# Two edits to a five-layer transformer stack on one core: other byte addresses for rows and weights, and one weight split moved ahead of each norm

## The reference

```
def rmsnorm(x, g):
    y = x * rsqrt(mean(x * x, -1) + 1e-6)
    return y * g
for i in range(4):
    h = rmsnorm(x, norm_mix_g[i])
    x = x + mixer_i(h)                       # h @ w_in ... @ w_out
    x = x + swiglu(rmsnorm(x, norm_ffn_g[i]), f_w13[i], f_w2[i])
# second block, on concat([meta, x])
h = h + mixer2(rmsnorm(h, norm_mix_w_2))     # h @ w_in (5792 columns)
h = h + swiglu(rmsnorm(h, norm_ffn_w_2), w_gate, w_up, w_down)
out = rmsnorm(h, norm_final_w)[:, 16:]
```

## Time and profile before

| | us |
|---|---|
| three runs | 1760.92, 1771.78, 1774.52 (median 1771.78) |
| the profiled execution, its own time | 1752.1 |
| its span, first to last instruction | 1750.3 |
| TensorE busy | 1691.5 (97%), mean granted clock 0.991 |
| VectorE busy | 1227.7 (70%) |
| ScalarE busy | 971.9 (56%) |
| HBM read | 288 MB, 165 GB/s over the span |

### The profile page before, as it was taken

How to read it: one execution, slowest core, us unless ns; L and a number is a source line. 1 busy time by engine, 2 the same in 40 slices (tenths; PEclk the granted TensorE clock), 3 DMA queues, 4 the chain that set the end, 5 groups by cost and what they waited for, 6 DMA issues and landing times.

```text
span 1750.3 us, 37337 instructions
## 1 busy us (share of the span) xinstructions
PE 1691.5 (97%) x13776; PEld 1599.1 (91%) x13776; DVE 1227.7 (70%) x2013; ACT 971.9 (56%) x1352; POOL 12.9 (1%) x20
## 2 busy tenths in 40 slices
PE   7999999999999999999999999999999999999997
PEld 7999999888999987569999999999999876799997
DVE  6887766586777587888776678776566665577764
ACT  4467745365775454206774446775454645468742
POOL 0000200000000000000000000000000000000000
PEclk9999999999999999999999999999999999999999
DMA  6567674433766554105666456667454432256662
GB/s 206 167 206 240 192 230 139 160 109 97 252 198 223 164 166 141 64 1 158 204 199 213 158 170 183 205 193 250 154 180 145 137 140 61 73 165 198 194 225 70
DMA packets 79545, 290.15 MB, mean 166 GB/s; under 512 B 9739, under 2 KB 12140, under 8 KB 79340
## 3 DMA queue, kind: packets, MB, share of 16 engines
q1 hardware_dynamic: 79468, 289.11, 52.2%
HBM read 288.03 MB, written 1.05 MB: 165 GB/s over the span
## 4 chain that ended last, share of the span: by engine, by line
PE 84%; DVE 11%; ACT 2%; issue 2%; DVEq 0%; DMA 0%; SPq 0%; ACTq 0%
PE bank L570 24%; PE bank L572 23%; PE bank L571 23%; DVE wlo L1516 3%; PE bank L858 2%; PE bank L845 1%; PE bank L799 1%; DVE conv_cv L1625 1%; DVE rinv L1522 1%; PE bank L954 1%; DVE hy_z L1765 1%; PE bank L1050 1%; ACT whi L1148 1%; PE bank L1060 1%; PE bank L1023 1%
## 5 line engine op out<-in xcount | busy, mean ns | idle before, releaser
L1148 ACT CAST whi<-raw 128x1024 fp32r<-128x1024 f32 (+1 forms) x490 | 539.3, 1102 | 328.4 <-PE bank L572 293.0
L570 PE MATMUL bank<-xq_h,whi 128*128 128x256 f32 x2384 | 666.9, 280 | 8.2 <-DVE wlo L1516 8.1
L571 PE MATMUL bank<-xq_h,wlo 128*128 128x256 f32 x2384 | 660.4, 277 | 0.0
L572 PE MATMUL bank<-xq_l,whi 128*128 128x256 f32 x2384 | 660.4, 277 | 0.0
L1516 DVE TENSOR_TENSOR wlo<-raw,whi 128x1024 fp32r<-128x1024 f32 (+1 forms) x491 | 629.9, 1283 | 5.4 <-ACT whi L1148 2.7
L570 PEld LDWEIGHTS bank<-xq_h,whi 128*128 128x128 f32 x2384 | 448.2, 188 | 19.3 <-DVE wlo L1516 12.7
L571 PEld LDWEIGHTS bank<-xq_h,wlo 128*128 128x128 f32 x2384 | 447.8, 188 | 1.5 <-issue 1.5
L572 PEld LDWEIGHTS bank<-xq_l,whi 128*128 128x128 f32 x2384 | 449.1, 188 | 0.0
L570 PE MATMUL bank<-ffn_hh,whi 128*128 128x256 f32 x880 | 242.9, 276 | 0.0
L571 PE MATMUL bank<-ffn_hh,wlo 128*128 128x256 f32 x880 | 242.9, 276 | 0.0
L572 PE MATMUL bank<-ffn_hl,whi 128*128 128x256 f32 x880 | 242.9, 276 | 0.0
(11 more groups left out here) (336 smaller groups left out, 2365.0 us busy)
## 6 DMA issues: line engine op xcount, KB each, us to landing
raw<-in_w SPq DMA_DIRECT2D x414, 512.0 KB, 3.6
raw<-in_w SPq DMA_DIRECT2D x80, 704.0 KB, 4.2
att_bias<-in_bias SPq DMA_DIRECT2D x4, 512.0 KB, 5.7
hy_w<-in_filt_w SPq DMA_DIRECT2D x8, 256.0 KB, 5.4
hy_decay<-in_decay SPq DMA_DIRECT2D x4, 512.0 KB, 4.4
mla_uq<-in_uq SPq DMA_DIRECT2D x1, 1152.0 KB, 5.4
x<-in_xT SPq DMA_DIRECT2D x1, 1024.0 KB, 5.9
out<-x SPq DMA_DIRECT2D x8, 128.0 KB, 2.0
```

Source lines behind the costliest of these rows:

```text
L570: pe.matmul(ps, whi[:, slot, wc], hi[:, k, cols], start=first, stop=False)
L571: pe.matmul(ps, wlo[:, slot, wc], hi[:, k, cols], start=False, stop=False)
L572: mm = pe.matmul(ps, whi[:, slot, wc], lo[:, k, cols], start=False, stop=last)
L1148: nc.scalar.copy(slices(whi, p % RING, k, to), raw_slices(p % RING, k, to)).then_inc(panel_hi, 1)
```

## The change

Two things. First the addresses: `whi` and `wlo` begin 4 elements (16 bytes) later than their allocation, two `align` tensors of 56 elements are put in, and the rows begin at 24 elements instead of 48. With the sizes in the code the weights come to 16 bytes above a multiple of 256 and the rows to 128 above one: weights 144 bytes behind the rows instead of 64, modulo 256. For the wide panels the first offset goes from 32 to 56 and from 16 to 40 elements, which gives the same 144. Second the order on DVE: at the nine norms named above `split_lo` of panel 3 stands in front of `norm_inv`'s wait for the root, and the first step of the product leaves it out (its split argument is None; the loop then starts at round 1). `in0`, whose first panels are split at the start, and the last norm stay as they were. No compute instruction is added or dropped.

```
-XROW_AT = 48
+W_AT = 4
+XROW_AT = 24
-L_FIRST = {SEQ: 2 * META, L: META}
+L_FIRST = {SEQ: 56, L: 40}
...
-    whi = sb("whi", [P, RING, SLOT], F32R)
-    wlo = sb("wlo", [P, RING, SLOT], F32R)
+    def weight_ring(name):
+        flat = sb(name, [P, W_AT + RING * SLOT], F32R)
+        return flat[:, W_AT:].rearrange("p (r s) -> p r s", r=RING)
+    whi = weight_ring("whi")
+    sb("align_weights", [P, 56])
+    wlo = weight_ring("wlo")
...
-    sb("align_rows", [P, 16])
+    sb("align_rows", [P, 56])
...
-    def steps(eng, ph, first, n, step, chain=None, per=0, ahead=4, loop=True):
+    def steps(eng, ph, first, n, step, chain=None, per=0, ahead=4, loop=True, split_early=0):
...
+        if split_early:
+            for j in range(4):
+                one(0, j, None if j < split_early else ph.k)
+            alone = 1
+        if rounds - alone > 1 and loop:
+            start = chain.n - alone * per if chain else 0
+            with eng.Fori(alone, rounds) as i:
...
+        def split_fourth(ph):
+            split_lo(ph, 0, 0, 0, ph.k)
-        def norm_inv(norm, cols):
+        def norm_inv(norm, cols, ph=None):
+            if ph is not None:
+                split_fourth(ph)
             dve.wait_ge(root_ready, norm + 1)
...
-            dve_steps(ph, 0, ph.n, step)
+            dve_steps(ph, 0, ph.n, step, split_early=1)
...
-            norm_inv(norm, A)
+            norm_inv(norm, A, PH[f"in{layer}"] if layer else None)
...
-            norm_inv(norm, A)
+            norm_inv(norm, A, PH[f"up{layer}"])
```

More of the change, by code:

```diff
@@ L1106, in _ @@
         assert norm + 1 == NORMS
-    def steps(eng, ph, first, n, step, chain=None, per=0, ahead=4, loop=True):
+    def steps(eng, ph, first, n, step, chain=None, per=0, ahead=4, loop=True, split_early=0):
         crossing = first + n == ph.n and ph.next_k != ph.k
         rounds = n // 4 - (1 if crossing else 0)
+        alone = 0
         def one(i, j, split):
             step(i, j, split)
-        if rounds > 1 and loop:
-            start = chain.n if chain else 0
-            with eng.Fori(0, rounds) as i:
+        if split_early:
[5 more added lines that the diff above has]
+            with eng.Fori(alone, rounds) as i:
                 if chain:
@@ L1125, in steps @@
         else:
-            for i in range(rounds):
+            for i in range(alone, rounds):
                 for j in range(4):
@@ L1498, in _, with dve_steps @@
         mask_bias()
-    def dve_steps(*args):
-        steps(nc.vector, *args, ahead=3)
+    def dve_steps(*args, **early):
+        steps(nc.vector, *args, ahead=3, **early)
     @block.vector
@@ L1607, in short_conv @@
             link(V.memset(cm["cu"][:], 0.0))
-            dve_steps(ph, 0, 8, scaled(ph, 0, 8, lambda j, m: cm["c"][:, m, :]))
+            dve_steps(ph, 0, 8, scaled(ph, 0, 8, lambda j, m: cm["c"][:, m, :]),
+                      split_early=1 if layer else 0)
             if layer == 0:
@@ L1719, in attention @@
                 evict(m, (ph.b0 + m) % 4)
-                split_lo(ph, 0, 0, m, K8)
+                if m:
+                    split_lo(ph, 0, 0, m, K8)
                 if m == 10:
@@ L1818, in multiply @@
                     dve.wait_ge(hs["Y"], 2 * n + f + 1)
-            dve_steps(ph, 0, 4, conv_step, link, 8)
+            dve_steps(ph, 0, 4, conv_step, link, 8, split_early=1)
             for p in range(4, 24):
@@ L1870, in decay_product @@
                 V.tensor_tensor(decay_of(h), decay_of(h), rx["e2"][:, h % 2, :], ALU.mult).then_inc(re["E"], 1)
-            dve_steps(ph, 0, 4, scaled(ph, 0, 4, lambda j, m: rt["t"][:, m, A]))
+            dve_steps(ph, 0, 4, scaled(ph, 0, 4, lambda j, m: rt["t"][:, m, A]), split_early=1)
             dve.wait_ge(re["lg"], 1)
@@ L2062, in _ @@
                      B if last else A)
-        norm_inv(norm, B)
+        norm_inv(norm, B, PH["in_ret"])
         norm += 1
@@ L2083, in _ @@
         residual(PH["w_o"], ("ffn_w2", 0), A, norm, A)
-        norm_inv(norm, A)
+        norm_inv(norm, A, PH["up4"])
         norm += 1
```

## The result

| | before | after |
|---|---|---|
| median of four runs each, same chip | 1766.35 (1756.25 to 1774.52) | 1802.39 (1801.35 to 1806.37) |
| profiled execution, its own time | 1752.1 | 1802.2 |
| its span, mean granted clock | 1750.3, 0.991 | 1800.4, 0.990 |

The ratio is 1.0211, with an interval of 1.0148 to 1.0274. The prediction was 1740 us, 1.8% less than the 1771.78 us that stood then as the median before. The clock is the same, so the 50.1 us between the two profiled executions aren't its doing.

The account below looks back on a forecast made before the run. TensorE was taken to bound the kernel, busy 1691.5 of 1750.3 us. The profiled 1752.1 less 7.8 (moved split) and 4.6 (new distance) gave 1739.7, say 1740 us, with an 8 in 10 range of 1696 to 1780.

Parts of the forecast that it names:

- What bounds the kernel: TensorE, busy 1691.5 of 1750.3 us; only less time for each matmul or fewer TensorE stalls can win time.
- two rates at one address pair: 256-column product matmuls take 113.3 or about 117.8 ns, drawn anew whenever TensorE stops and starts.
- the 19.7 us between profile and median: Median above profiled time, laid to about three of five feed-forwards at 117.8 ns, 6.8 us each.
- Part 1: At nine norms, panel 3's subtraction moved in front of the norm removes TensorE stalls: 7.8 us saved.
- the stall was also the draw: Without panel 3's stall, 117.8 ns could last through a feed-forward: 6.8 us lost against about 0.9 saved.
- Part 2: The 144-byte distance leaves product matmuls at 113.3 ns: 4.6 us saved, none of it from the five feed-forwards.
- in_ret: Part 2's term for the 272-column products: 286 matmuls by 5.5 ns, 1.6 us saved.
- the nearest row: The steady 113.3 ns of three feed-forwards, taken as the rate when weights and rows don't disturb each other.
- a worse distance everywhere: Rival: 144 bytes disturbs rows in each matmul; 1780 us at 117.8 ns, range 1778 to 1830; chance 0.14.
- A floor below 113.3: Rival: 144 bytes lowers each matmul to, say, 109 ns, saving 39 us, to 1701 us; chance 0.2.
- the layout does nothing: Rival: two rates remain, stalls are saved but fewer draws happen; 1744 to 1778, middle 1765 us; chance 0.24.
- The late norm: Rival: the moved split delays nine norms by at most 1 us each; 1740 to 1744 us; chance 0.02.

Follow-up runs that it names:

- order_only: The kernel after with before's addresses (128, 64), keeping the new order on DVE: 1770.01 us, ratio to before 1.0036.
- layout_only: The kernel after with the old order on DVE at all nine norms, keeping the new addresses: 1801.45 us, ratio to before 1.0203.
- d64_rows80: The kernel after with rows of x, hidden layer and mixers' outputs moved to 80 modulo 256, weights kept at 144: 1743.19 us, ratio to before 0.9873.

## Why the prediction was wrong

**What bounds the kernel: right.** TensorE is busy for 97% of the span in both, and the time followed the nanoseconds of one matmul. The reading of two rates at one address pair, drawn when TensorE starts and kept until it stops, held: order_only had up0, up1 and up4 at 117.7 throughout and up2 and up3 at 113.3. Priced as the prediction did it, three of five give 1744 + 20 = 1764; its profiled execution took 1765.9. That the draws also make up the 19.7 us between profile and median fits the runs, though none tests it directly: where feed-forwards draw no rate, medians lie within 3 us of the profiled execution and the spread falls to 2 to 8 us. One detail was misread. The better rate doesn't begin after the stall at panel 3 in every feed-forward: in front of that stall 4.00 us hold 36 matmuls in up0, up1 and up3, but 38 in up2 and up4, which were at the better rate already. So a stall is a new draw, and not what brings the better rate.

**Part 1, 7.8 us: right in its sum.** 8.3 us measured, at addresses without draws in the feed-forwards. The added wait costs 0.18 us at up0, inside idle time. The shares differ from those foreseen: the feed-forwards and in3 alone gained 7.9 where 5.9 were counted, in part because the stalls were longer there (1.24 us at up0, not 1.06), and in2 lost part of its gain to panel 4, as the prediction had it. That the sums come within 0.5 us is some luck. The remark that the stall was also the draw was needed: at (128, 64) the same edit came out at 1.0036 [0.9999, 1.0072].

**Part 2, a gain of 4.6 us: this step failed.** It says "I take 113.3 for every stretch, that is, the new distance removes the worse rate and leaves the better one". Measured were 118.3 to 120.2 in the feed-forwards and 116.7 at the least anywhere. The price from the windows: the 1584 matmuls in each feed-forward (44 panels of 24 and 16 of 33) by 5.0, 5.1, 6.7, 6.6 and 6.9 ns are 7.9 + 8.1 + 10.6 + 10.5 + 10.9 = 48.0 us. The 46 matmuls in front of each panel 3 were already at 117.8 before in up0, up1 and up3, which takes off 3 x 46 x 4.5 ns = 0.6, so 47. With 8 us won by the split, the remaining products must account for 50.1 - 47 + 8 = 11 us, by difference and not measured each for itself. The one term with the right sign was in_ret: 1.3 of the 5.5 ns that were expected. That row wasn't one of a distance of 64 bytes to begin with, since a third of its matmuls had a distance of 0, so its excess said nothing sure of that distance.

What was wrong in the reasoning was the choice of the nearest row. The steady 113.3 was a state of the pair (128, 64), one of its two; nothing in the trace tied it to the absence of a conflict at another pair. Both ends named beside it, 106.7 and 5% over 113.3, were as near. And the change was described by the distance alone, while the runs show that the distance decides nothing by itself: 144 gives 113.3 at (128, 240) and 118 to 120 at (144, 0), and 64 gives a steady 113.3 at (144, 80) and a drawn one at (128, 64).

**The rivals.** The one on the slower side, a worse distance everywhere, is what came, with its own turning point: past 1% slower from 118.8 ns, and 1791 at 119.0. It had 0.14, with "no stretch with 256 columns is above 118.0" against it; but those rows spoke of the pair (128, 64) alone. A floor below 113.3 (chance 0.2) found no support: with 256 columns no steady stretch of any kernel here is faster. The Trainium skill, "TensorE: Matmul & The Clock Gate", section "Wait — 56ns, not 53.3ns?", gives N/2.4 GHz plus about 2.5 ns, an estimated 109.2 ns for 256 columns; no run here reached it. That the layout does nothing (0.24) is refuted by layout_only, 1.0203: only SBUF addresses differ between d64_rows80 and the kernel after, and the rate of the same matmul differs by up to 6.7 ns. The Trainium skill says in "SBUF — State Buffer", section "SBUF: two separate sides", that TensorE never waits for anyone at SBUF; what the prediction drew from it, that the addresses change nothing, doesn't hold here. Whether TensorE waits for another engine or its own two streams disturb each other, no run shows. The late norm (0.02) cost nothing that can be seen: in the kernel after, the subtraction runs right up to the norm in in2, up2 and up3, and no weight load waits for DVE behind the norms of up2 and up3.

**What stays open.** Why a pair of addresses has its rate, and what picks among two or three rates at one pair when TensorE starts. The table isn't enough for a rule: with the three pairs under it, it holds 16 of the 256 pairs in steps of 16 bytes, most seen in one run. That positions count modulo 256 bytes, and not modulo 512 or more, is assumed and was not tested. What separates 272 columns from 256 is open too, as no wide product has a single pair.

## What to carry to other kernels

When matmuls of one shape run at two rates at one clock, count them per window before anything else, and treat the SBUF addresses of weights and rows as a pair to be measured, with one profiled run for each of several pairs; don't argue from their distance. An edit that removes a stall can look worthless while each restart draws a rate: fix the addresses first, then judge the order (a ratio of 1.0036 here with draws, 8.3 us gained without them).

## What the runs showed of the hardware

- The time of one 128x128x256 `fp32r` matmul with its weight load at full clock took one of several steady values, 113.3, about 116.6, 117.8, 118.3, 119 or 120.0 ns, by the positions of weights and rows (given modulo 256 bytes). A step of 16 bytes in the rows took it from 113.3 at (128, 240) to 119.6 at (128, 224).
- At some pairs the rate isn't fixed. At (128, 64) it is 113.3 or 117.8, at (144, 0) 116.7, 118.3 or 120.0, for over 1400 matmuls in a row in the windows of order_only and layout_only. At (128, 240) and (144, 80) every feed-forward shown was at 113.3.
- The products with 272 columns didn't follow those with 256. The kernel after has 124.6 ns in in_ret where before had 125.9, while its 256-column matmuls in the feed-forwards are 4% to 6% slower. As these products run through four pairs each, with low rows at another distance, no run tells the width from the pairs.
